# Two reorderings at the ends of the gates' stage of a two-block transformer kernel

## The reference, cut to what matters

```python
gates = jax.nn.sigmoid(gate_pre.reshape(B, L, N_BRANCH, D_MODEL) + gate_bias[l])
merged = (gates[:, :, 0] * (y_a @ w_branch[l, 0])
          + gates[:, :, 1] * (y_b @ w_branch[l, 1])
          + gates[:, :, 2] * (y_c @ w_branch[l, 2]))
x = x + rms_norm(merged @ w_out[l], g[1])
h = rms_norm(x, g[2])
mem_n = rms_norm(mem, mem_norm[l])
x = x + rms_norm(memory_cross_attention(h, mem_n, xa_wq[l], xa_wkv[l], xa_wo[l]), g[3])
```

## Time and profile before

| | |
|---|---|
| median of 3 runs | 1871.67 us (1870.27 to 1873.55) |
| the profiled execution's own time | 1871.13 us |
| its span in the profile | 1869.3 us |
| mean granted TensorE clock | 0.973 |
| TensorE busy | 1783.7 us, 95% of the span |
| VectorE, ScalarE, GpSimd busy | 1158.4, 807.7, 334.4 us |
| moved by DMA | 195.97 MB, mean 105 GB/s |
| chain that ended last | TensorE 81%, VectorE 8%, ScalarE 5%, GpSimd 2% |

### The profile page before, as it was taken

The page is one execution under the profiler, slowest core; times in us unless marked ns, Lnnn a source line. Parts: engine busy times, 40 slices in busy tenths (PEclk is TensorE's granted clock), DMA queues, the critical chain, the costliest instruction groups (busy, mean ns, idle before and its releaser), DMA issues.

```text
span 1869.3 us, 24902 instructions
## 1 busy us (share of the span) xinstructions
PE 1783.7 (95%) x9919; PEld 1481.3 (79%) x9919; DVE 1158.4 (62%) x1846; ACT 807.7 (43%) x1396; POOL 334.4 (18%) x287
## 2 busy tenths in 40 slices
PE   7999999999999998989999999899978999999998
PEld 5778877779997877778888888797756688999887
DVE  6778854479885365455777742465456469888322
ACT  4433344354443454343443432336357545655221
POOL 2014501031101140041111110230010032332100
PEclk9999999999999999989999999899979899999999
DMA  5222322236654431112332333241321154775521
GB/s 193 83 87 91 102 91 79 68 96 158 153 131 158 146 112 46 46 58 90 112 91 90 93 100 100 68 136 46 98 69 33 35 154 125 191 193 143 183 90 57
DMA packets 62356, 195.97 MB, mean 105 GB/s; under 512 B 7386, under 2 KB 10074, under 8 KB 62112
## 3 DMA queue, kind: packets, MB, share of 16 engines
q1 hardware_dynamic: 48960, 162.51, 27.3%
q0 software_dynamic: 12704, 31.34, 7.5%
q10 hardware_dynamic: 576, 0.52, 0.1%
HBM read 188.05 MB, written 6.29 MB: 104 GB/s over the span
## 4 chain that ended last, share of the span: by engine, by line
PE 81%; DVE 8%; ACT 5%; issue 4%; POOL 2%; DMA 1%; SPq 0%; DVEq 0%; POOLq 0%; ACTq 0%
PE ps L405 25%; PE ps L407 24%; PE ps L406 24%; PE ps L410 3%; PE ps L3362 2%; POOL sums L453 1%; DVE ws_l L341 1%; ACT ws_h L333 1%; PE ps L3379 1%; POOL x L1836 1%; DMA x<-in_x 1%; DVE tmp L851 0%; DVE P L3623 0%; PE ps L3374 0%; DVE mg_l L917 0%
## 5 line engine op out<-in xcount | busy, mean ns | idle before, releaser
L341 DVE TENSOR_TENSOR ws_l<-raw,ws_h 128x1024 fp32r<-128x1024 f32 x228 | 315.4, 1389 | 341.4 <-ACT ws_h L333 341.0
L405 PE MATMUL ps<-h_h,ws_h 128*128 128x512 f32 (+2 forms) x1140 | 447.2, 392 | 23.6 <-DVE h_l L584 9.6
L406 PE MATMUL ps<-h_l,ws_h 128*128 128x512 f32 (+2 forms) x1140 | 435.9, 382 | 0.0
L407 PE MATMUL ps<-h_h,ws_l 128*128 128x512 f32 (+2 forms) x1140 | 435.3, 382 | 0.0
L333 ACT ACTIVATE ws_h<-raw 128x1024 fp32r<-128x1024 f32 x228 | 238.8, 1053 | 282.5 <-PE ps L407 274.6
L405 PEld LDWEIGHTS ps<-h_h,ws_h 128*128 128x128 f32 x1140 | 218.1, 191 | 79.0 <-issue 14.8
L407 PEld LDWEIGHTS ps<-h_h,ws_l 128*128 128x128 f32 x1140 | 218.4, 192 | 43.3
L406 PEld LDWEIGHTS ps<-h_l,ws_h 128*128 128x128 f32 x1140 | 219.5, 193 | 39.7
L453 POOL TENSOR_TENSOR sums<-sums,tmp 128x512 f32<-128x512 f32 (+1 forms) x44 | 60.0, 1363 | 433.0 <-ACT tmp L445 410.7
L407 PE MATMUL ps<-fb_h,ws_l 128*128 128x256 f32 x476 | 133.8, 281 | 0.0
L405 PE MATMUL ps<-fb_h,ws_h 128*128 128x256 f32 x476 | 133.7, 281 | 0.0
(11 more groups left out here) (534 smaller groups left out, 3499.4 us busy)
## 6 DMA issues: line engine op xcount, KB each, us to landing
raw<-in_ffn_up SPq DMA_DIRECT2D x88, 512.0 KB, 3.6
raw<-in_w_merge SPq DMA_DIRECT2D x36, 512.0 KB, 4.2
raw<-in_ffn_down SPq DMA_DIRECT2D x22, 512.0 KB, 3.5
raw<-in_w_down SPq DMA_DIRECT2D x22, 512.0 KB, 3.5
raw<-in_w_hy SPq DMA_DIRECT2D x12, 512.0 KB, 4.2
raw<-in_w_sc SPq DMA_DIRECT2D x12, 512.0 KB, 3.5
s<-in_ffn_up SPq DMA_DIRECT2D x17, 256.0 KB, 4.1
s<-in_ffn_up POOLq DMA_DIRECT2D x17, 256.0 KB, 4.8
```

What stands on the lines that cost most here:

```text
L341: dve.e.tensor_tensor(w.lo, raw[n % NRAW][:], w.hi, ALU.subtract).then_inc(*lo_made.says(("lo", n)))
L405: pe.e.matmul(o, a.hi, b.hi, start=start, stop=False, skip_group_check=True)
L406: pe.e.matmul(o, a.hi, b.lo, start=False, stop=False, skip_group_check=True)
L407: return pe.e.matmul(o, a.lo, b.hi, start=False, stop=stop, skip_group_check=True)
```

## The change

At the start of the stage the memory's squares are made two tiles at a time: four squares of 128 x 512 into four buffers (`acc`, `T[4]`, `T[5]`, `eighth`), none of which is used twice, three additions of 128 x 512 on GpSimd, and two products by ones, one for each half of `acc`, that sum into one bank. At the end of the stage, in VectorE's order, four of the eight low parts of the memory are moved ahead of `gated(10, 0)`, the split of the last branch chunk ahead of `gated(10, 1)`, and the other four low parts behind the next split.

```diff
+    MEM_SQUARES = (acc, T[4][:, 0:L], T[5][:, 0:L], eighth)
...
@@ merge_pe
         branch(0, main)
-        total("mem", 256, bank(("sum", "mem"), rings["seven"]), 8, False)
+        o = bank(("sum", "mem"), rings["seven"])
+        pe.wait_ge(("added", "mem", 3))
+        for i in range(2):
+            last = mm32(o[:, 0:256], ones[:], acc[:, 256 * i:256 * i + 256], i == 0, i == 1)
+        last.then_inc(*products.says(("sum", "mem"), ("done", ("sum", "mem"))))
         gates(2)
@@ merge_act
-        blocks, slots = Follow(chunk_act), Ring(place, (4, 5), ("gone", ("qk", 3, 1)))
+        blocks = Follow(chunk_act)
...
         blocks.next(8)
-        act.wait_ge(("mem", 0), ("mem", 1))
-        for i in range(8):
-            square("mem", i, me(i), 256, "meta", False, slots)
+        for i in range(4):
+            act.wait_ge(("mem", i // 2), ("sum", "meta"), ("gone", ("qk", 3, 1)), ("yb", 3))
+            act.e.activation(MEM_SQUARES[i], (mgh, mgl)[i // 2][:, 6 + i % 2, :], ACT.Square).then_inc(
+                *squared.says(("sq", "mem", i)))
         sigmoid(1, 0)
@@ merge_dve
+        def memory_lo(tiles):
+            for i in tiles:
+                dve.wait_ge(("mn hi", i))
+                dve.e.tensor_tensor(mn[:, i, :].lo, me(i), mn[:, i, :].hi, ALU.subtract).then_inc(
+                    *dve_part.says(("mn", i)))
...
             if s < LATE:
                 row_and_first(s + 1)
+            if s == LATE:
+                memory_lo(range(4))
             gated(s - 1, 0)
...
                 second_sum(s + 1)
                 other_half(s + 1)
+            if s == LATE:
+                n = splits["dve"] = fence["merged"]
+                until["dve"] = fence["n"]
+                split_lo(n + 1)
             gated(s - 1, 1)
             if s < LATE:
                 branch_half(s + 1, 0)
-        for i in range(8):
-            dve.wait_ge(("mn hi", i))
-            dve.e.tensor_tensor(mn[:, i, :].lo, me(i), mn[:, i, :].hi, ALU.subtract).then_inc(*dve_part.says(("mn", i)))
-        n = splits["dve"] = fence["merged"]
-        until["dve"] = fence["n"]
-        split_lo(n + 1)
         c21(LATE)
         split_lo(n + 2)
+        memory_lo(range(4, 8))
         used["dve"] = n
@@ merge_pool
-        for i in range(1, 8):
-            add_square(pool, added_pool, "mem", i, 256)
+        for i in range(1, 4):
+            pool.wait_ge(("sq", "mem", 0), ("sq", "mem", i), ("added", "mem", i - 1) if i > 1 else None)
+            pool.e.tensor_tensor(acc, acc, MEM_SQUARES[i], ALU.add).then_inc(*added_pool.says(("added", "mem", i)))
```

## The result

The changed kernel took 1862.51 us in the median of six runs (1858.06 to 1865.73), beside 1871.12 for the kernel before in its six: a ratio of 0.9951, 95% interval 0.9935 to 0.9968. The prediction was 1863.2 and faster. The profiled execution had a span of 1856.3 us, 13.0 less than before's; the prediction's sum was 8.5, and where the other 4.5 came from is told there too.

The account below looks back on a forecast made before the run. TensorE, busy 1783.7 of 1869.3 us, was taken to bound the kernel. Gains of 3.63 and 4.87 make 8.5 us off the median of 1871.67, giving 1863.2; own range 1861.5 to 1865, wider range 1860.5 to 1867.

Parts of the forecast that it names:

- TensorE's two waits and the slow products behind them: At the gates stage's start and end, removing 5.4 us of waits and the low clock behind gains 3.63 and 4.87 us.
- Full pace after the waits go: At both ends of the stage, products follow each other every 0.234 us, with a clock of 1.00 from 405 to 600.
- The second rival: At both places the waits go but products stay slow; only 5.3 us of idle is won: 1866.4, chance 0.08.
- The second product by ones: At the stage's start, the squares' total takes two products, the extra one costing TensorE about 0.43 us (bounds 0.4 and 0.59).
- VectorE's path: At the stage's start, VectorE taking turns with GpSimd's additions starts L1580 at 406.85, later than ScalarE's path at 405.2.
- The covers: At the stage's start, weights for the first and second tile are ready about 0.4 us before TensorE needs them.
- the first rival: At the stage's start, additions hold VectorE longer and low parts come after TensorE, costing 1 to 2 us: 1864.7, chance 0.2.
- The first gap's squares: At the stage's start, four 512-wide ScalarE squares wait for no addition and are done 3.4 us after they begin.
- The four low parts and the split: At the stage's end, 1.38 and 1.22 us of work fit VectorE's two 1.78 us idle times, 0.4 and 0.5 over.
- What is late next: At the stage's end, VectorE's chain up to the output product stays tied to TensorE, keeping 0.9 us of cover.
- The slower rival: Outside the two waits, eight new falls of the clock, about 1.6 us each, make the kernel slower: 1875.5, chance 0.02.
- The third rival: At one of the two places another wait is last, so only one gain is left: 1866.8 or 1868.0, chance 0.06.

Follow-up runs that it names:

- single-part kernels: Two kernels, each the kernel before with one half of the change: new squares, additions and total, ratio 0.9990; VectorE's new order at the stage's end, ratio 0.9967.
- the kernel with eight: Changed kernel without GpSimd's additions, TensorE summing the four square buffers with eight products by ones; 1864.56 us in one run.
- fold: Changed kernel with a fourth GpSimd addition, 256 wide, folding the two halves of the sum, and one product by ones; 1863.88 us in one run.
- eight late: Changed kernel with all eight low parts of the memory behind the second split, none ahead of the gated product; 1863.30 us in one run.
- split behind the gated product: Changed kernel with the last branch chunk's split right behind the gated product of step 10 instead of ahead of it; 1863.68 us in one run.
- squares only: Changed kernel with VectorE's order at the stage's end as before; 1869.43 us in 12 runs, ratio 0.9990.
- the second series: The changed kernel run once more with no edit; 1860.46 us in 5 runs, ratio 0.9944.
- low parts only: Kernel before with VectorE's new order at the stage's end, its squares, additions and total untouched; 1867.42 us in 5 runs, ratio 0.9967.

## Why the prediction was right

- **TensorE's two waits and the slow products behind them are the price.** Right: the stage became 8.48 us shorter, 3.59 and 4.89, against 3.63 and 4.87. The single-part kernels show that the two gains stand apart and add.
- **Full pace after the waits go.** Right at both places, in all profiles where the wait was gone: the granted clock there is 1.00 in each. The second rival (the clock does not come back) is out.
- **The second product by ones, 0.43 us.** Right: two take 0.87, and the kernel with eight pays 0.42 for each of the six more.
- **VectorE's path is the later one, by turns with GpSimd.** Right in kind, shown by the kernel without additions. The size does not follow from its own words. Before, the last of VectorE's two sums was

```profile
403.14 1.64 DVE L1568 TENSOR_TENSOR gt_f<-gt_f,h_l 128x1024 f32<-128x1024 f32 x1
```

It ended at 404.8, of which 0.54 and 0.42 us were stretches by the small additions (1.76 and 1.64 against 1.22), so without any addition the sums would end at about 403.8. Three full turns of 1.3 us on top give 407.7, and not the 406.85 of the prediction, which holds only 3.0 us of turns and does not say what takes the rest off. With 407.7 the weights would have been ready at 410.1, 0.4 us after TensorE's 409.68. The runs showed 1.1, 0.5 and 1.0, 2.6 us in all, and L1586 at 406.34 on that scale. That TensorE had no wait for VectorE here is in part luck: the assumption of full turns, carried through, forecast one. The covers are 1.0 and 0.9 us and not 0.4, and the first rival, to which I had given 0.2, did not come.
- **The first gap's squares.** They took 2.2 us, under the bound of 3.4.
- **The four low parts and the split fit in VectorE's idle times.** Right: 0.43 and 0.64 left, against 0.4 and 0.5.
- **What is late next.** Right: the output product keeps 0.95 us of cover (0.9 forecast), and the kernel with eight late low parts shows what lies behind it.
- **The rest of the kernel.** The span less A and B was 1691.6 us before and 1687.1 after. That is the 4.5 us which the first profile has over the sum. Over all thirteen profiles this remainder runs from 1687.1 to 1695.9. The two profiles of the changed kernel have the lowest two (1687.1 and 1687.7), but three kernels that hold both parts of the change and differ from it by less than a microsecond in A and B (fold, eight late, split behind the gated product) have 1692 to 1693. The remainder goes with the clock. The granted clock's shortfall, summed over windows of 10 us outside 400 to 600 (10 us times one less the clock, the last window left out), is 44.4 us before, 35.8 after and 37.5 in its second profile, and 47.9 in the kernel with the largest remainder (squares only). The unchanged kernel shows it alone: of its 17 runs fourteen took 1870.5 to 1873.2 us at a mean granted clock of 0.971 to 0.973, the other three 1862.3 to 1866.5 at 0.975 to 0.979. So a median says which of these were drawn more often. The means are 1870.4 for those 17 and 1861.8 for the eleven of the changed kernel: 8.6 us, good to about 2 us by the scatter of the runs (an estimate), with no sign of a gain beyond the stage's 8.5. That the first medians differ by 8.61 where the sum was 8.5 is therefore luck to some extent; the second series had 11.0, and its 1860.46 lies just under the 1860.5 that the prediction named as the wider range's lower end. Why the clock falls more often in some executions is left open; no run tested it.

The slower rival needed eight new falls of the clock; the shortfall outside the stage was smaller in both profiles after, not larger. The third rival is out too: both terms of the sum were there.

## What to carry to other kernels

Price a wait of the bounding engine with the slow products behind it, and read both off the timeline as the start that full pace would need: here 5.4 us of waiting cost 8.9, the 8.48 gained and the 0.44 that the second product by ones takes. Look for the room in the idle times of the engine that is late, just ahead of where it waits for the bounding engine; work that nobody needs soon goes there or behind, and what the next product needs goes first. When buffers make two engines go step by step, fewer and wider steps into buffers of their own free the first engine, but look at what the second engine's steps do to a third: here GpSimd's additions stretched VectorE's work by 2.6 us. And where executions of one kernel differ by more than the gain, measure the stage itself in the profiles.

## What the runs showed of the hardware

- A 1.8 us wait of TensorE was followed by no slow product and one of 2.5 us by 1.5 us of loss, in two profiles each, at the same place, in kernels that differ only in VectorE's order there; the 2.25 us one at the stage's start was followed by slow products too (granted clock 0.66 from 412 to 417 before, 0.70 with the low parts only; A of 167.06 and 167.09). By the Trainium skill, "TensorE: Matmul & The Clock Gate", section "What's actually happening", the throttled clock is the default and activity is what releases it. The trace agrees in this: the clock was 0.50 from 570 to 572 behind the wait of 2.5 us, and 1.00 again from 574 with TensorE busy throughout.
- GpSimd's additions held back VectorE's instructions with two SBUF inputs: 1.22 us became 2.33 beside a 512-wide addition, and an addition went from 1.3 to 2.1, while an eviction from PSUM between them kept its 0.68. By the Trainium skill, "SBUF — State Buffer", section "Who interferes with whom", a VectorE instruction with two SBUF inputs contends with a GpSimd instruction that reads SBUF. The trace agrees (2.33 against 1.22 us without additions). The time lost per meeting, 0.5 to 1.1 us, is less than the addition's whole 1.3: it is what was left of the addition when VectorE came to it.
